# A two-layer hybrid decoder step: the first key/value chunk before the norm's sum, and the second MLP's input rows written elsewhere, one behind each square

## The reference, cut to what matters

```
def rmsnorm(x, g):
    y = xf * lax.rsqrt(jnp.mean(xf * xf, axis=-1, keepdims=True) + RMS_EPS)
    return y * g

x = x + hgrn_mix(rmsnorm(x, norm_mix[0]), ...)                       # layer 0: gated linear recurrence
x = x + square(relu(rmsnorm(x, norm_mlp[0]) @ w_up[0])) @ w_down[0]  # "mlp0"
kv = rmsnorm(x, norm_kv) @ w_kv                                      # "kv": 1024 -> 1536
h  = rmsnorm(x, norm_mix[1])
x = x + nsa_attend((h @ w_q), kv, caches) @ w_o                      # layer 1: sparse attention, "nsa_out"
x = x + square(relu(rmsnorm(x, norm_mlp[1]) @ w_up[1])) @ w_down[1]  # "mlp1"
y = rmsnorm(x, norm_final)
```

## Time and profile before

| | |
|---|---|
| median of 3 runs | 2033.1 us (2032.31 to 2034.29) |
| profiled execution | 2028.27 us |
| its span, first to last instruction | 2026.7 us |
| TensorE busy | 1909.3 us (94%) |
| VectorE, ScalarE, GpSimd busy | 836.0, 482.7, 702.5 us |
| mean granted TensorE clock | 0.973 |

### The profile page before, as it was taken

How to read it: one execution, slowest core, us unless ns; L and a number is a source line. 1 busy time by engine, 2 the same in 40 slices (tenths; PEclk the granted TensorE clock), 3 DMA queues, 4 the chain that set the end, 5 groups by cost and what they waited for, 6 DMA issues and landing times.

```text
span 2026.7 us, 27941 instructions
## 1 busy us (share of the span) xinstructions
PE 1909.3 (94%) x10570; PEld 1584.6 (78%) x10570; DVE 836.0 (41%) x1483; ACT 482.7 (24%) x998; POOL 702.5 (35%) x830
## 2 busy tenths in 40 slices
PE   7999999899999999999989989799857899999998
PEld 6888888778888888888856668687535788888887
DVE  2555555425534343210157754244420345252523
ACT  4344343221101010200244533233310211010102
POOL 2324332234434343300046654342030524444442
PEclk9999999799999999999989999899987899999999
DMA  5322222112222222213850008896996022222221
GB/s 147 96 64 66 75 64 90 38 42 83 84 83 84 84 84 91 97 62 93 224 126 1 2 1 188 204 189 163 289 312 237 0 81 86 83 83 84 83 83 43
DMA packets 164855, 207.24 MB, mean 102 GB/s; under 512 B 14049, under 2 KB 101714, under 8 KB 164594
## 3 DMA queue, kind: packets, MB, share of 16 engines
q1 hardware_dynamic: 146834, 186.80, 31.9%
q10 hardware_dynamic: 16544, 14.98, 2.3%
q0 software_dynamic: 1344, 3.67, 0.5%
HBM read 194.33 MB, written 18.42 MB: 105 GB/s over the span
## 4 chain that ended last, share of the span: by engine, by line
PE 80%; DVE 7%; ACTq 3%; issue 2%; SPq 2%; DMA 2%; ACT 2%; POOL 1%; DVEq 0%; POOLq 0%
PE ps L1218 34%; PE ps L1032 12%; PE ps L1069 11%; PE ps L1356 4%; PE ps L1349 2%; PE ps L1109 2%; DMA stream<-in_cache_nsa_kv 2%; ACTq L2054 2%; PE ps L1084 2%; PE ps L1405 1%; PE ps L1427 1%; PE ps L1445 1%; DVE scratch L2388 1%; ACTq L417 1%; DVE big L2348 1%
## 5 line engine op out<-in xcount | busy, mean ns | idle before, releaser
L1218 PE MATMUL ps<-big,stream 128*128 128x260 f32 x1792 | 393.7, 382 | 0.0
L1218 PEld LDWEIGHTS ps<-big,stream 128*128 128x128 f32 x1792 | 340.5, 190 | 52.3
L835 POOL TENSOR_TENSOR stream<-stream 128x512 f32<-128x512 f32 x64 | 93.6, 1462 | 540.7 <-DMA stream<-in_w_mlp_up 262.2
L1218 PE MATMUL ps<-scratch,stream 128*128 128x260 f32 x1024 | 238.7, 386 | 6.8 <-DVE scratch L2375 4.7
L1069 PE MATMUL ps<-h,stream 128*128 128x260 f32 x1024 | 234.8, 384 | 0.0
L1218 PEld LDWEIGHTS ps<-scratch,stream 128*128 128x128 f32 x1024 | 194.7, 191 | 42.9 <-DVE scratch L2375 10.5
L1069 PEld LDWEIGHTS ps<-h,stream 128*128 128x128 f32 x1024 | 190.2, 190 | 31.1 <-issue 4.6
L1218 PE MATMUL ps<-h,stream 128*128 128x260 f32 x768 | 181.8, 385 | 3.9 <-ACT h L1749 3.1
L1218 PEld LDWEIGHTS ps<-h,stream 128*128 128x128 f32 x768 | 145.9, 191 | 28.4 <-issue 3.8
L1032 PE MATMUL ps<-h,stream 128*128 128x260 f32 x640 | 142.8, 386 | 1.7 <-DVE h L2747 1.7
L1032 PEld LDWEIGHTS ps<-h,stream 128*128 128x128 f32 x640 | 123.0, 192 | 21.3 <-DVE h L2747 2.1
(11 more groups left out here) (372 smaller groups left out, 2902.3 us busy)
## 6 DMA issues: line engine op xcount, KB each, us to landing
stream<-in_w_mlp_up SPq DMA_DIRECT2D x16, 2048.0 KB, 8.3
stream<-in_w_mlp_down SPq DMA_DIRECT2D x16, 2048.0 KB, 7.9
stream<-in_cache_nsa_kv SPq DMA_DIRECT2D x128, 256.0 KB, 6.1
stream<-in_w_hgrn_in SPq DMA_DIRECT2D x32, 512.0 KB, 6.8
stream<-in_cache_nsa_kv SPq DMA_DIRECT2D x114, 128.0 KB
stream<-in_cache_nsa_kv ACTq DMA_DIRECT2D x114, 128.0 KB
stream<-in_cache_win_kv SPq DMA_DIRECT2D x16, 512.0 KB
out<-in_cache_win_kv SPq DMA_DIRECT2D x8, 1022.0 KB
```

The source lines that it names most:

```text
L835: nc.gpsimd.tensor_tensor(weight_sum(j, half, S3), A11, A21, ALU.subtract).then_inc(fast["wsum"], 1)
L1218: m = nc.tensor.matmul(bank(w, b), weight(k), columns(k), start=(start and k == 0), stop=(stop and k == HK - 1), skip_group_check=True)
```

## The change

It has two parts. First, TensorE's list behind mlp0 now begins with chunk 0 of kv, whose first eight products wait each for its own row of h; the norm's sum stands behind that chunk, and chunks 1 to 11 follow. Second, mlp1 reads its input from rows 0 to 7 of big, which attention no longer uses by then. Its gains are written there early, and the hidden rows of its quarters 0 and 2, which stood in those rows, go to h. VectorE's operand sums for mlp1 stand between the residual additions as before mlp0.

```
-        hid = [parts(0), parts(2 * KD)]
+        mlp_in = {"mlp0": h, "mlp1": parts(0)}
+        hid = {"mlp0": [parts(0), parts(2 * KD)], "mlp1": [h, parts(2 * KD)]}
...
-            def chunk_products(slab, cols, k_rows, rhs, c_local, c, before):
+            def chunk_products(slab, cols, k_rows, rhs, c_local, c, before, row_wait=None):
...
                     for k in range(k_rows):
+                        if row_wait and a == 0:
+                            row_wait(k)
                         m = nc.tensor.matmul(pair(c)[0:n1, a, :], w[:, k, P * c_local:P * c_local + n1],
...
-            norm_sum("attn", squares)
-            pe.wait_ge(norm["out"], out_count["kv"])
-            dense("kv", 3, h, KD, 512)
+            for n in range(12):
+                j = slab_base["kv"] + n // 4
+                if n % 4 == 0:
+                    pe.wait_ge(slab_in[slab_slot(j)], slab_count(j))
+                chunk_products(slot[slab_slot(j)], 512, KD, h, n % 4, chunk_base["kv"] + n, 0,
+                               lambda k: pe.wait_ge(norm["out"], out_count["mlp0"] + k + 1) if n == 0 else None)
+                if n == 0:
+                    norm_sum("attn", squares)
...
-            norm_act("mlp1", squares, added("nsa_out"), late=[(GAIN_MLP + KD, h)])
-            mlp(PER)
+            norm_act("mlp1", squares, added("nsa_out"), early=[(GAIN_MLP + KD, mlp_in["mlp1"])])
+            mlp("mlp1", PER)
...
-                operand_sums(h[:, 2 * k:2 * k + 2, :], h_sums[:, :, k, :], tsum_base[name] + 4 * k)
+                operand_sums(mlp_in[name][:, 2 * k:2 * k + 2, :], h_sums[:, :, k, :], tsum_base[name] + 4 * k)
...
-            residual("nsa_out")
-            for k in range(HK):
-                sums_of_h("mlp1", k)
+            residual("nsa_out", lambda k: sums_of_h("mlp1", k // 2 - 1) if k % 2 and k >= 3 else None)
+            sums_of_h("mlp1", HK - 1)
             norm_dve("mlp1")
```

10 lines of the change are left out of this document (5 added, 5 removed).

## The result

| | before | changed |
|---|---|---|
| median | 2027.3 us (19 runs, 2023.45 to 2034.29) | 2019.35 us (19 runs, 2015.74 to 2028.61) |
| profiled execution | 2028.27 us | 2018.3 us |
| its span | 2026.7 us | 2016.7 us |
| mean granted TensorE clock | 0.973 | 0.975 |

What follows compares the result with a forecast made beforehand. TensorE, 80% of the chain, bounds the kernel where it idles or runs at its lower clock, here at two handoffs. Savings of 2.14 and 5.77 make 7.9 us: 2033.1 - 7.9 = 2025.2 us, range 2020.4 to 2029.4 (8 in 10).

Steps and rivals of the forecast that it cites:

- the base: Whole kernel: the time the saving is taken from, 2033.1 us, the median of the runs then at hand.
- an offset that stays: Whole kernel: the runs' median lies 4.8 us above the profiled execution's 2028.27, and would do so after the change.
- Rival one: Second MLP's start: VectorE and GpSimd do not collide; 12.3 us saved in all, 2020.8 us; chance 0.10.
- rival two: Second MLP's start: TensorE's clock falls in new gaps of 1.2 and 0.9 us; 3.9 saved, 2029.2; chance 0.15.
- The cover of 1.5 us: First handoff: time between the first scaling's end, about 872.0, and TensorE's need of it at 873.55.
- D: Second MLP's start: a TensorE product forecast to stop 1.2 us before its last row, awaiting VectorE's sums.
- B: Second MLP's start: a TensorE product forecast to stop 0.9 us before its last row, awaiting VectorE's sums.
- the mark: Second MLP's start: second half of D, first product needing the second temporary; forecast at 1618.15 instead of 1623.92, 5.77 saved.
- Three: Key/value projection or attention: the 2.14 us vanish, at the third chunk or later; 2027.3 us; chance 0.08.
- Four: Attention: moved by 2 us, its handoffs keep the clock low longer; slower, 2040.4 us; chance 0.05.

Runs made afterwards that it cites:

- e3: The kernel before, unchanged, run again as if it were another kernel: 2028.01 us, ratio 1.0004 to the kernel before.
- e4: The changed kernel with two key/value chunks ahead of the norm's sum in place of one: 2029.84 us, ratio 1.0016 to the kernel before.
- e8: The kernel before, with GpSimd's second-slab weight sums waiting for VectorE's sixteen operand sums: 2022.91 us, ratio 0.997 to the kernel before.
- e7: The changed kernel with all sixteen operand sums back behind the residual additions, gains still early: 2028.01 us, ratio 0.9989 to the kernel before.
- e5: The changed kernel, with GpSimd's second-slab weight sums waiting for VectorE's sixteen operand sums: 2017.56 us, ratio 0.9938 to the kernel before.
- e6: The changed kernel with the second MLP's reciprocal moved behind the first pair's temporaries and third quarter: 2018.58 us, ratio 0.9952 to the kernel before.
- e14: One more profile of the kernel before, unchanged: key compression 41.49 us, span 2030.9 us.
- e2: The kernel before with only the second MLP's early inputs in other rows and its moved sums: 2023.4 us, ratio 0.9987 to the kernel before.
- e13: The kernel before with ten unread products added behind the last key/value chunk: 2033.84 us, ratio 1.0031 to the kernel before.

## Why the prediction was right or wrong

The time is outside the range, 2019.35 us against 2020.4 to 2029.4, while the difference is right: 7.9 us forecast, 7.1 measured (4.7 to 9.7).

**The step that failed** is the base: "I take this as an offset that stays: 2033.1 - 7.9 = 2025.2". There is no such offset. The three runs lie close together (2032.31 to 2034.29), but in 19 runs the same kernel has a median of 2027.3 and goes from 2023.45 to 2034.29, and in the later sets of runs its medians are 2027.8 (35 runs), 2026.9 (30), 2029.0 (17) and 2028.0 (17), with single executions from 2018.36 to 2037.98. The three were high ones: of the other 115 executions of this kernel on record, 16 are at 2032.3 us or above. If executions were independent, three such in a row would come in 0.3% of cases (16/115 cubed), so something may have held these three up; what it was stays open. With the 19 runs as the base, 2027.3 - 7.9 = 2019.4, what came out; that it fits to a tenth is luck, since without the three the median is 2026.1, and the interval of the gain is 5 us wide. The profiled execution (2028.27) was the better base of the two, by chance: that of e3 lies 7.3 us below its own median. The scatter runs with the granted clock. Over the 19 runs of the changed kernel, time and mean clock correlate at -0.85 (in the four later sets of the kernel before at -0.81 to -0.89), from 0.969 at 2028.61 us to 0.976 at 2015.74; 0.007 of 2020 is 14 us, and the times differ by 12.9.

**The range** was built from rivals alone and held nothing for the base. All of it was taken from 2033.1. Rival one's gain of 12.3 gives 2020.8 there, and rival two's 3.9 gives 2029.2; the range was then written as 2020.4 to 2029.4, for which the text has no reason. The measured time is below either lower end.

**Part one** was right in each step. Idle behind the last product 0.79 us (0.8 forecast), norm's sum 1.92 us and not slowed, no gap before the third chunk, first scaling 14.71 us behind the last addition's start (871.3 - 856.8 = 14.5 forecast), 2.16 us saved (2.14). The cover of 1.5 us was 1.3; e4 took it away and lost 5.66. What the sum did not have is that the lower clock sometimes follows the old gap (e8, 1.57 us more).

**Part two** too. Waits of 1.47 us in D (1.2 forecast) and 0.80 in B (0.9); the last sum ends at 1610.30, 10.79 us behind the last addition's end (10.9); the mark 15.77 us behind its start (15.8), with a wait of 1.43 us before it (1.2); 5.8 us saved up to the mark and 5.69 to the addition behind it (5.77). e7 shows that the gains by themselves do not carry this and the sums' order is needed, e5 that the rest is GpSimd's share, e6 that the reciprocal stood on the path. The prediction took the length of the stretch before as given, with the 5.81 us of its last 18 products, and named only the first fall of the clock in it. In e3 the second did not come, and against that profile part two gives 4.1 us and not 5.7.

**The rivals.** One (no collision) is refuted for the changed kernel by 1.49 and 1.38 us a sum, and confirmed as a mechanism by e5, which reaches its 11.4 us to the mark. Two (the clock falls in the new gaps) is refuted for this kernel: 1.00 in the whole stretch, and no fall there in the other profiles with this order of the sums. It had more for it than its text said: the kernel before fell to 0.50 behind gaps of 1.09 and 0.90 us (1616.5 us, above). And what it set against itself, the 2.98 us without a fall, holds in five profiles of six. Three (the third chunk stalls) is refuted by the timeline, and e4 shows its price. Its other half, a loss later in attention, was there in this profile, 3.3 us in the key compression, but e14 has 4.2 of it without any change. Four (slower, with attention at a lower clock) is refuted by the time. Its sign did show in one slice, the 21st, 7 in place of 8, which is that key compression; attention from its last unit on took 345.17 us against 346.72.

**The chances** fared better than the time: faster had 0.84, and faster it is. But it was counted as a time below 2029.0, from a base of 2033.1, and the kernel before itself lies below that line with 2027.3. So it was the right answer by a wrong line.

## What to carry to other kernels

Before a forecast is put on a base, ask how far single executions of that kernel scatter: three runs 2 us apart said nothing of a spread of 9 to 19 us, and the base's error (5.8 us) was as large as the effect. At a handoff between stages, look for the engine that feeds the next stage's operands, take out of the gap all that can be made earlier, and then look at which other engine's instructions slow it there; one wait on GpSimd gave 4.5 us on top of the 5.7 that eight gains and eight sums gave by moving. How many chunks may be pulled ahead of a norm's sum depends on the banks that are free until its result is there: here, with two pairs of banks, one chunk gained 2.2 us and a second cost 5.7 of waiting.

## What the runs showed of the hardware

**Alternation.** Beside GpSimd's weight sums (1.27 us alone, 1.33 to 1.46 there) VectorE's sums of two operands take turns with them: in the changed kernel's last eight, one starts every 1.4 us from the second on, where one takes 0.43 in e5, with GpSimd held back. The kernel before gained 6.0 us (2.2 to 9.7) from that one wait (e8).

**The clock behind gaps.** In the second handoff of the kernel before it fell in a stretch with gaps of 2.17 us and two of 0.47, and again behind gaps of 1.09 and 0.90 us (in e3, with 1.23 and 0.90, it did not). It fell in e4 behind one of 5.66 us and in e7 in one of 3.86. With gaps of 0.79, 1.47 and 0.80 us in the changed kernel it stayed at 1.00. Behind the single gap of 2.98 us of the first handoff it stayed at 1.00 in five profiles (before, e2, e3, e13, e14) and was at 0.50 in the sixth (e8). So the length of one gap does not tell by itself whether the clock falls, and the same code does either.

**Two levels of one stretch.** The key compression took 37.2 to 37.3 us in six profiles and 40.6 to 42.4 in eleven, by the place at which the clock fell, with the same instructions. Layer 0 (451.5 to 456.3 us) and the rest of attention (345.2 to 351.7) vary as well, with the same code, and the time goes with the mean clock. So two profiles of this kernel are not compared by their spans, but stretch by stretch.
